# A two-layer encoder step in float32: three reduced products for each matmul, or one direct float32 product, with a six-slot weight ring

## The reference

```python
for layer in range(DEPTH):                      # DEPTH is 2
    hp = rms_norm(xp, norm_mix[layer])
    yp, sp = even_prompt(hp, *w)                # layer 0; odd_prompt in layer 1
    xp = xp + yp
    xp = xp + conv_ffn(xp, norm_ffn[layer], ffn_w_in[layer], ...)

def even_prompt(h, w_in, table, w_out):
    qa, ka, va, qb, kb, vb = split(h @ w_in)    # 1024 x 3072
    # 8 heads of banded softmax attention (A), 8 of stick-breaking attention (B)
    return concat([oa, ob]) @ w_out

def conv_ffn(x, g, w_in, conv_w, conv_b, w_out, past):
    u = rms_norm(x, g) @ w_in                   # 1024 x 5632
    c = conv_b + sum(conv_w[i] * up[:, i:i + T] for i in range(3))
    a, b = split(c, 2)
    return (silu(a) * b) @ w_out                # 2816 x 1024
```

## Time and profile before

| | |
|---|---|
| time, median of 3 runs | 3545.11 us (3538.51 to 3546.26) |
| span of the profiled execution | 3550.5 us |
| PE busy | 3300.5 us (93%) |
| DVE busy | 1479.8 us (42%) |
| ACT busy | 1051.1 us (30%) |
| POOL busy | 585.6 us (16%) |
| mean granted TensorE clock | 0.953 of full speed |

### The profile page before, as it was taken

One profiled execution on the slowest core, in us unless ns is written; L12 is line 12 of the kernel. 1 busy time (PEld: TensorE's weight loads), 2 busy tenths in 40 slices (PEclk: granted clock), 3 DMA queues, 4 the chain that ended last, 5 costly groups with the idle time before them and its releaser, 6 DMA issues. The chain is left out here.

```text
span 3550.5 us, 49644 instructions
## 1 busy us (share of the span) xinstructions
PE 3300.5 (93%) x17488; PEld 2767.6 (78%) x17488; DVE 1479.8 (42%) x2714; ACT 1051.1 (30%) x2417; POOL 585.6 (16%) x352
## 2 busy tenths in 40 slices
PE   5999999999989999999999989989897999999997
PEld 4777777766579999999966556655456999999996
DVE  4233366567153343333441434434324343443335
ACT  3333355454132221222210033334404222222222
POOL 2111111110032222222300000000003223222220
PEclk8999999899999999999999989978898999999998
DMA  2111110000101111111011100000001111111111
GB/s 85 37 37 37 37 39 30 30 22 16 51 30 43 48 43 43 43 49 43 31 47 36 32 10 8 4 4 12 24 29 39 47 43 42 49 43 43 43 42 51
DMA packets 52798, 127.65 MB, mean 36 GB/s; under 512 B 11760, under 2 KB 19968, under 8 KB 52640
## 3 DMA queue, kind: packets, MB, share of 16 engines
q1 hardware_dynamic: 44160, 108.33, 9.2%
q0 software_dynamic: 5312, 16.80, 1.4%
q10 hardware_dynamic: 3168, 0.18, 0.1%
HBM read 111.52 MB, written 13.76 MB: 35 GB/s over the span
## 5 line engine op out<-in xcount | busy, mean ns | idle before, releaser
L1053 PE MATMUL ps<-hh,wh 128*128 128x384 f32 (+1 forms) x2112 | 697.5, 330 | 38.4 <-POOL hl L113 33.0
L1053 PE MATMUL ps<-hl,wh 128*128 128x384 f32 (+1 forms) x2112 | 697.2, 330 | 0.0
L1053 PE MATMUL ps<-hh,wl 128*128 128x384 f32 (+1 forms) x2112 | 696.4, 330 | 0.0
L1180 POOL TENSOR_TENSOR wl<-raw,wh 128x1024 fp32r<-128x1024 f32 x132 | 330.1, 2501 | 1123.6 <-ACT wh L1106 1123.6
L1053 PEld LDWEIGHTS ps<-hh,wh 128*128 128x128 f32 x2112 | 400.9, 190 | 42.6 <-issue 42.6
L1053 PEld LDWEIGHTS ps<-hh,wl 128*128 128x128 f32 x2112 | 401.0, 190 | 0.0
L1053 PEld LDWEIGHTS ps<-hl,wh 128*128 128x128 f32 x2112 | 399.4, 189 | 0.0
L1223 DVE TENSOR_SCALAR gates<-u,par 128x1090 f32<-128x1090 f32 x88 | 74.6, 848 | 772.6 <-ACT tail L1131 772.6
L225 PE MATMUL pot<-hh_mix,wh_mix 128*128 128x384 f32 (+1 forms) x576 | 220.0, 382 | 30.5 <-ACT q_next L261 16.1
L1106 ACT ACTIVATE wh<-raw 128x1024 fp32r<-128x1024 f32 x132 | 138.8, 1051 | 341.0 <-PE pot L1072 193.3
L225 PE MATMUL pot<-hl_mix,wh_mix 128*128 128x384 f32 (+1 forms) x576 | 195.3, 339 | 0.0
(11 more groups left out here) (224 smaller groups left out, 5774.4 us busy)
## 6 DMA issues: line engine op xcount, KB each, us to landing
raw<-in_ffn_w SPq DMA_DIRECT2D x132, 512.0 KB, 3.2
w<-in_w SPq DMA_DIRECT2D x64, 256.0 KB, 2.5
w<-in_w SPq DMA_DIRECT2D x12, 512.0 KB, 3.6
w<-in_w_out SPq DMA_DIRECT2D x16, 256.0 KB, 2.6
strip<-in_bias POOLq DMA_DIRECT2D x5, 640.0 KB, 4.1
x<-in_x SPq DMA_DIRECT2D x4, 768.0 KB, 9.3
out_y<-x SPq DMA_DIRECT2D x2, 1536.0 KB, 6.3
out_bv<-vt POOLq DMA_DIRECT2D x4, 512.0 KB, 3.0
```

Source lines behind the costliest of these rows:

```text
L1053: mm = e.matmul(bank[:, 0:b - a], w[:, n % 3, k * P:(k + 1) * P], x[:, k, a:b], start=k == 0 and first, stop=k == KT - 1 and w is m.wl)
L1180: e.tensor_tensor(m.wl[:, n % 3, :], m.raw[:, n % 3, :], m.wh[:, n % 3, :].bitcast(F32), ALU.subtract).then_inc(self.low, 1)
```

## The change

Every split goes. The norms of layer 0 and of the feed-forward blocks write one float32 tile `hn`; the gate writes one float32 tile `g`; the weights are multiplied as they come from HBM. Each group of three float32r matmuls becomes one matmul with float32 operands. The weight ring of the feed-forward has six slots instead of three, each refilled when PE has used it; the tile of convolution parameters is loaded by POOL's queue instead of SP's. In layer 0 the q, k and v weights come in units of 128x1024 instead of halves of 128x512. The ACT and POOL work of splitting is gone.

```diff
-            if self.split:
-                if i >= 4:
-                    e.wait_ge(self.low_p if i % 2 else self.low_v, (i - 4) // 2 + 1)
-                out = m.tmp[:, i % 4, 0:b - a]
-            else:
-                out = self.dst(k, a, b)
-            e.scalar_tensor_tensor(out, self.src(k, a, b), g, m.rms[:, c, 0:b - a],
+            e.scalar_tensor_tensor(self.dst(k, a, b), self.src(k, a, b), g, m.rms[:, c, 0:b - a],
                                    ALU.mult, ALU.mult).then_inc(self.normed, 1)
-            if self.split and i % 2 == 1:
-                self.low(e, i - 1, self.low_v)
         e.wait_ge(self.normed, len(self.items))
...
-            if self.latent:
-                mm = e.matmul(m.pnext[:, 0:b - a], m.w[:, (self.base // 3 + w) % self.ring, k * P:(k + 1) * P],
-                              self.source(what)[:, k, a:b], start=k == 0, stop=last)
-            else:
-                half = 2 * w + k // 4
-                if c == 0 and k % 4 == 0:
-                    e.wait_ge(self.low, p * 6 + half + 1)
-                at = slice(k % 4 * P, k % 4 * P + P)
-                for x, y, start in ((m.hh, m.wh, k == 0), (m.hl, m.wh, False), (m.hh, m.wl, False)):
-                    mm = e.matmul(m.pnext[:, 0:b - a], y[:, half % 3, at], x[:, k, a:b], start=start,
-                                  stop=last and y is m.wl)
+            mm = e.matmul(m.pnext[:, 0:b - a], m.w[:, (self.base // 3 + w) % self.ring, k * P:(k + 1) * P],
+                          self.source(what)[:, k, a:b], start=k == 0, stop=last)
...
+    def load(self, e, n):
+        e.dma_start(self.m.raw[:, n % 6, :], self.weights[n]).then_inc(self.raw_in[n % 6], 16)
...
     def sync(self, e):
         m = self.m
-        for s in range(self.RING):
-            e.dma_start(m.raw[:, s, :], self.weights[s]).then_inc(self.raw_in[s], 16)
-        e.dma_start(m.par[:, 0, :, :], self.params[0]).then_inc(self.par_in[0], 16)
-        e.wait_ge(self.low, 1)
-        e.dma_start(m.raw[:, 0, :], self.weights[3]).then_inc(self.raw_in[0], 16)
-        with e.Fori(0, (GROUPS - 1) // 2) as i:
...
+            self.load(e, n)
...
+        for n in range(6, 10):
+            e.wait_ge(self.up, 3 * (n - 5))
+            self.load(e, n)
+        with e.Fori(0, 4) as i:
             for s in range(12):
-                n = 4 + s
-                e.wait_ge(self.low, i * 12 + n - 2)
-                e.dma_start(m.raw[:, n % 3, :], self.weights[bass.ds(i * 12 + n, 1)].rearrange("a p c -> (a p) c")).then_inc(self.raw_in[n % 3], 16)
...
-            e.dma_start(m.raw[:, n % 3, :], self.weights[n]).then_inc(self.raw_in[n % 3], 16)
+                self.wait_used(e, i, 4 + s)
+                n = 10 + s
+                e.dma_start(m.raw[:, n % 6, :], self.weights[bass.ds(i * 12 + n, 1)].rearrange("a p c -> (a p) c")).then_inc(self.raw_in[n % 6], 16)
+        for n in range(58, 66):
+            self.wait_used(e, 4, n - 54 + 0)
+            self.load(e, n)
+    def gpsimd(self, e):
+        m = self.m
+        for g in range(GROUPS):
+            if g >= 2:
+                e.wait_ge(self.conv, 4 * (g - 1))
+            e.dma_start(m.par[:, g % 2, :, :], self.params[g]).then_inc(self.par_in[g % 2], 16)
+    def wait_raw(self, e, i, n):
+        e.wait_ge(self.raw_in[n % 6], i * 32 + 16 * (n // 6 + 1))
...
     def pe_up(self, e, i, g, norm=None):
...
-            e.wait_ge(self.low, i * 12 + n + 1)
+            self.wait_raw(e, i, n)
...
                 for k in range(KT):
-                    for x, w, first in ((m.hh, m.wh, True), (m.hl, m.wh, False), (m.hh, m.wl, False)):
-                        mm = e.matmul(bank[:, 0:b - a], w[:, n % 3, k * P:(k + 1) * P], x[:, k, a:b],
-                                      start=k == 0 and first, stop=k == KT - 1 and w is m.wl)
+                    mm = e.matmul(bank[:, 0:b - a], m.raw[:, n % 6, k * P:(k + 1) * P], m.hn[:, k, a:b],
+                                  start=k == 0, stop=k == KT - 1)
...
     def pe_down(self, e, i, g, last=False):
...
-        e.wait_ge(self.glow, i * 4 + 2 * g + 2)
+        e.wait_ge(self.gate, i * 4 + 2 * g + 2)
...
-                e.wait_ge(self.low, i * 12 + n + 1)
+                self.wait_raw(e, i, n)
...
                 for k in range(2):
                     col = (mt % 4) * 2 * P + k * P
-                    for x, w, first in ((m.gh, m.wh, True), (m.gl, m.wh, False), (m.gh, m.wl, False)):
-                        mm = e.matmul(bank[:, 0:b - a], w[:, n % 3, col:col + P], x[:, 2 * par + k, a:b],
-                                      start=k == 0 and first, stop=k == 1 and w is m.wl)
+                    mm = e.matmul(bank[:, 0:b - a], m.raw[:, n % 6, col:col + P], m.g[:, 2 * par + k, a:b],
+                                  start=k == 0, stop=k == 1)
...
+    def sc_silu(self, e, i, f):
+        m = self.m
+        e.wait_ge(self.conv, i * 8 + 2 * f + 1)
+        if f:
+            e.wait_ge(self.gate, i * 4 + f)
+        e.activation(m.sa[:, :], m.ca[:, :], ACT.Silu).then_inc(self.silu, 1)
...
     def sc_up(self, e, i, g):
-        m = self.m
         for tile in range(4):
-            n = tile if g == 0 else 4 + 6 * (g - 1) + tile
             for c in range(3):
                 self.sc_leave(e, i, g, tile, c)
-                if c == 0:
-                    self.sc_high(e, i, n + 2)
-                    if tile % 2 == 0 and (g or tile):
-                        self.sc_ghigh(e, i, 2 * g + tile // 2 - 1)
             if tile == 3:
                 e.wait_ge(self.left, i * 24 + 12 * g + 12)
                 dst = self.tails[0] if g == 0 else self.tails[bass.ds(i * 2 + g, 1)].rearrange("a p t c -> (a p) t c")
-                e.dma_start(dst, m.tail[:, g % 2, :, :]).then_inc(self.tails_out, 16)
+                e.dma_start(dst, self.m.tail[:, g % 2, :, :]).then_inc(self.tails_out, 16)
             if tile % 2:
-                f = 2 * g + tile // 2
-                e.wait_ge(self.conv, i * 8 + 2 * f + 1)
-                if f:
-                    e.wait_ge(self.glow, i * 4 + f)
-                e.activation(m.sa[:, :], m.ca[:, :], ACT.Silu).then_inc(self.silu, 1)
...
-                m.hh = sb(ctx, f"hh{layer}", [P, KT, T], F32R)
-                m.hl = sb(ctx, f"hl{layer}", [P, KT, T], F32R)
-                norm = norm_of_x(f"norm_ffn{layer}", GAIN_FFN[layer], split=(m.hh, m.hl))
-                m.raw = sb(ctx, f"raw{layer}", [P, 3, 1024])
-                m.wh = sb(ctx, f"wh{layer}", [P, 3, 1024], F32R)
-                m.wl = sb(ctx, f"wl{layer}", [P, 3, 1024], F32R)
+                m.hn = sb(ctx, f"hn_ffn{layer}", [P, KT, T])
+                norm = norm_of_x(f"norm_ffn{layer}", GAIN_FFN[layer], lambda k, a, b: m.hn[:, k, a:b])
+                m.raw = sb(ctx, f"raw{layer}", [P, Ffn.RING, 1024])
                 m.u = sb(ctx, f"u{layer}", [P, 2, T + 2])
                 gates = sb(ctx, f"gates{layer}", [P, 3 * T])
                 m.ca, m.cb, m.sa = (gates[:, i * T:(i + 1) * T] for i in range(3))
-                m.sq, m.tmp = ring4(gates), ring4(gates[:, 4 * 384:8 * 384])
+                m.sq = ring4(gates)
                 m.rms = sb(ctx, f"rms_ffn{layer}", [P, 3, 384])
-                m.gh = sb(ctx, f"gh{layer}", [P, 4, T], F32R)
-                m.gl = sb(ctx, f"gl{layer}", [P, 4, T], F32R)
+                m.g = sb(ctx, f"g{layer}", [P, 4, T])
...
-            attention_scratch(ctx, 0, 3, 512)
-            m.wh, m.wl = sb(ctx, "wh_mix0", [P, 3, 512], F32R), sb(ctx, "wl_mix0", [P, 3, 512], F32R)
+            attention_scratch(ctx, 0, 3, 1024)
...
-                    for i in range(3):
-                        e.dma_start(m.w[:, i, :], io.w0[i]).then_inc(m.w_in[i], 16)
-                    with e.Fori(0, 16) as i:
-                        for s in range(3):
-                            e.wait_ge(st.low, i * 3 + s + 1)
-                            e.dma_start(m.w[:, s, :], io.w0[bass.ds(i * 3 + 3 + s, 1)].rearrange("a p c -> (a p) c")).then_inc(m.w_in[s], 16)
...
+                    weight_stream(e, m, [(io.w0, 1024, 24), (io.w0_out, 512, 16)], 3)
```

185 lines of the change are left out of this document (29 added, 156 removed).

## The result

The changed kernel takes 3854.9 us (median of 4 runs, 3853.9 to 3857.4), the kernel before 3545.7 us on the same chip. The ratio on record is 1.088, 95% interval 1.0864 to 1.0895 (the quotient of the two medians is 1.087): some 8.8% slower, 28 us less than the 3883 forecast and inside the range of 3840 to 3915.

A forecast was written before the change was run, and what follows sets the result against it. PE was taken to bound the kernel (busy 93% of the span). Terms 357 - 16 - 40 - 16 + 53 = +338 us on the 3550.5 us span gave 3888, less 5.4 for the median 3883 us; range 3840 to 3915.

The forecast's parts named there:

- (2): Feed-forwards: PE's 20 waits for the fifth down bank, 15.9 us in all, would go: -16 us.
- (5): Projection products in layer 0's pairs: +33 us for four A pairs, 5 of the B pairs' 25 hidden, together +53 us.
- Cost of one product: On PE, a direct product takes 0.611 us, three reduced ones 0.495 (up) or 0.499 (down).
- item 1: Feed-forward products after the first 24: 178.5 us more for a layer, +357 us for both.
- Starts of the feed-forwards: From DVE's last add to the first tile's third cut, each start becomes 38.8 us: -18.8 and -21.0, together -40 us.
- Start of layer 0: PE begins at 29.8, third cut at 49.3 instead of 71.29: -22 us, other 48 products +6, together -16 us.
- the step by which waits for exponentials hide a part of the price: In the B pairs, 6.9 us of waits for ACT's exponentials take part of the 25 us; 5 taken off.
- Ring, parameters: Feed-forward weight slots, parameter loads and lost ACT and POOL split work cost PE nothing outside the starts: 0.
- the lower clock in long float32 stretches: Rival: clock 0.97 instead of 1.00 in direct products adds 59 us, 3940 us; with other new waits, chance 0.09.
- the halved price: Rival: a direct product takes 0.305 us, time near 2,800 us; no chance beyond the faster rival's 0.02.
- the hidden fillers: Rival: PE does all pairs' longer projection products in its pauses, pair term 0, 3830 us; chance 0.06.

The follow-up runs named there:

- The fastest version: Kernel before with PE's loop written out, splits behind the squares, two adds ahead of DVE's last convolution operation, POOL's split made to wait: 3498.1 us, ratio 0.9873.

## Why the prediction was right

The sign, the size and the mechanism held: a direct float32 product costs PE more than three reduced ones, and where PE sets the end that is what the change costs. Two terms were off in size: the gaps that the change takes out of the feed-forwards were larger (2), and the pairs lost less (5). By its steps:

1. *Cost of one product.* Direct: 0.611 forecast, 954.1 us / 1560 products = 0.6116 measured. Old way: 0.495 and 0.499 forecast. The fastest version has a body of 777.6 us without a wait, 0.4984 for each product, and its matmul starts stand 0.166 us apart. So item 1 should have been 954.1 - 777.6 = 176.5 us for a layer instead of 178.5; the single distance of 11.88 us in the earlier trace rows began with a cut taken some 0.1 us late.

2. *Wait for the down bank.* It went, as forecast. But it was mis-sized, the largest error in the feed-forwards. 791.94 - 777.58 = 14.4 us of the body before were gaps and not 8: ten bank waits cost 788.3 - 777.6 = 10.7 us, and four turns of PE's loop cost 3.7, which I had passed over. The idle time in the earlier trace rows counts from a modelled end of the matmul, 0.79 us of it; from start to start the gap is 1.13 us instead of 0.17, the next distance is 0.28, and the body loses 1.07. The run with the loop written out and the last run show the two apart. 176.5 - 14.4 = 162.1, and 162.2 was measured.

3. *Starts of the feed-forwards.* -19.8 and -21.2 measured, -18.8 and -21.0 forecast. 7.2 us of the first lie between DVE's last add and ACT's first square, which the run with the moved splits shows.

4. *Start of layer 0.* -14.7 measured, -16 forecast. PE's first projection product came at 30.4 (29.8 forecast), but ACT's third cut of q at 51.9, not 49.3. PE's rows there:

```profile
39.58 6.93 PE L173 MATMUL pot<-hn,w 128*128 128x384 f32 x16 [3.76 <-ACT q_next L191]
...
47.23 1.08 PE L173 MATMUL pot<-hn,w 128*128 128x322 f32 x3 [0.72 <-DVE q_next L192]
```

The projection goes through one bank here, so the second cut waits until ACT has taken the first, and ACT comes to that only behind its part of the norm of the third cut. It begins 9.2 us after the first cut; in layer 1, which I took for the pattern and whose cuts go to banks of their own, 7.9. That and the 0.7 us ahead of the third cut are the 2 us. The other 48 products with what follows made up part of it: +4.7, not +6.

5. *Pairs.* +39.7 measured, +53 forecast: the term with the largest miss. In the changed kernel the A pairs are 28.4 us longer (7.1 each, where 8.3 were forecast) and the three B pairs 10.9. The run with only these products direct has +44.4, so 4 to 5 us came back with the splitting: PE's wait for ACT's copy of q at the openings is 23.6 us in all in that run, 23.1 before and 19.1 after. I had left the openings unchanged. The price by itself: A pairs 32.6 of 33.3, in full; B pairs 12.2 of 25, half of it gone where I took a fifth. I had argued that waits would take it, and they took little of it. The three B pairs by windows, before and in the run with only these products direct and the loop written out:

```profile
456.80:771.80 315.00, 296.31 (x1674) 237.50 (x1674) 205.10 (x298) 169.03 (x289) 43.29 (x36) 0.92 0.09 27
```

```profile
496.70:823.80 327.10, 310.03 (x1458) 199.59 (x1458) 204.35 (x297) 167.85 (x288) 43.27 (x36) 0.96 0.08 26
```

The stretch grew by 12.1 us and PE's busy time by 13.7, so its idle time fell by less than 2 us. The granted clock rose from 0.92 to 0.96: of the 315 us some 50 were at the lower level of 1.2 GHz before, some 26 of the 327 in this run. Half of these 24 us is what such a change gives back to an engine that works throughout, 12 us, and about what is missing from the 25. That is an estimate from the two rows, and no run tried the clock by itself. So the step by which waits for exponentials hide a part of the price did not hold, and that the B pairs lost less than their full price was right by luck.

6. *Ring, parameters.* Zero, as forecast and as the run with three slots shows.

Layer 1 gave 5.6 us that no step had: before, 143 us of it ran at a mean clock of 0.93, after, 135 at 1.00. Over the runs of this study the same stretch took 135.4 to 142.9 us with the same code. The profiled execution of the kernel before is the odd one: its layer 1 up to the last projection add took 852.7 us, in eleven other traces, with reduced and with direct products, it was 845.6 to 847.9 (in two more 836.6 and 836.9). So it belongs to the clock of that execution, and not to the change.

The sum of the misses: feed-forwards 17, pairs 13, layer 1 and end 6, and the three starts balance: the 36 us between 338 and 302. All but the starts missed to the same side, so no luck made the sum good; that the three starts cancel to 0.1 us is luck. Of the rivals, the lower clock in long float32 stretches is refuted (1.00 over 954 us), the halved price too (0.611, not 0.305), and the hidden fillers came true nowhere: the A pairs paid in full, and what the B pairs did not pay goes with the clock and not with waits. The divisor of two for FP32_LOW_HIGH that the Trainium skill gives in Perfetto Trace Analysis, section Engine Utilization, doesn't hold for a whole direct product of this kernel; 0.305 us is what each of its two records takes.

## What to carry to other kernels

Before replacing several cheap matmuls by one dear one, find both on the same tile shapes in the trace and divide distances between the takers of results by the number of products; here two rows each gave the two prices within 1%, their difference within 3%, and the sign for sure. Size a wait by what the stage would take without it and not by the idle time in a row: here 14 gaps with 10.6 us of idle time in their rows were worth 14.4 us. And before an operation of DVE is moved, look what POOL does at that moment: an order that was harmless can put POOL's operation first, on the path.

## What the runs showed that I had not expected

- DVE and POOL hold each other up when both inputs of DVE's operation lie in SBUF. DVE's convolution operation (two SBUF inputs) takes 1.35 us alone and 3.04 to 3.37 when POOL's split of 2.40 started first; POOL's takes 3.08 when DVE's did. Moving two adds cost 12 to 41 us by it, of the 41 about half through the clock, which fell behind PE's longer waits; with a wait of POOL ahead of its splits the same move made each body 10.6 us shorter.
- A turn of PE's loop costs 0.7 to 1.0 us between reduced matmuls and nothing between direct ones. With another program ahead of it, a second gap of 1.8 to 3.0 us came up some matmuls later, 25 us in all with what the clock lost. In that gap the trace has one packet of the instruction queue, 16 KB, at about 1248.2, and PE goes on at 1250.49. The Trainium skill, Runtime: NRT & Kernel Launch, section Instruction fetch mechanics, says that a taken branch out of the fetched window must wait for a fetch; the packet agrees with it, but it proves little: in the kernel before such a packet stands at 1195.8, just behind the edge whose gap ends at 1195.4, and no second gap follows. Why the gap's size depends on the program ahead was not tried.
- In the B pairs of layer 0 the granted clock was 0.92 on the mean with reduced products and 0.96 with direct ones, and about half of the direct products' price did not show there. In the A pairs it was 0.96 with both, and the price showed in full.
- Layer 1's stretches of short matmuls differ from run to run by up to 10 us through the granted clock. Differences of that size can be read by stage only, and not from a total.
